# Four blocks of token tiles instead of three in a decoder step: samples in the second, recurrence over eight heads, weight stream opened per stage group

## The reference, cut to what matters

```
h = rms_norm(x, n_mix_pre) * (1 + sc1) + sh1
bg, cg, hin, q, k, v, r, ga, gb, alow = split(h @ w_in)
branch_a = (bg * short_conv(cg * hin)) @ w_proj_a
log_a = log_sigmoid(alow @ w_alpha + b_alpha) / 16
o, s_new = gla_chunked(q, k, v, log_a, state)       # recurrence over tokens, 4 heads
branch_b = (rms_norm(o) * silu(r)) @ w_proj_b
m = (sigmoid(ga) * branch_a + sigmoid(gb) * branch_b) @ w_out
x = x + g1 * rms_norm(m)
h = rms_norm(x) * (1 + sc2) + sh2
# PEER: 8 heads, two top-16 lists of 128 keys each, top 16 of the 256 sums = 128 experts a token
act = gelu(u_tab[expert] . h);  y = sum(gate * act * v_tab[expert])
x = x + g2 * rms_norm(y)
```

## Time and profile before

| | |
|---|---|
| device time, median of 3 runs | 4959.62 us (4947.52 to 4969.03) |
| the profiled execution | 4954.23 us, its span 4952.4 us |
| PE, DVE, POOL, ACT busy | 69%, 53%, 35%, 20% of the span |
| granted clock of PE, mean | 0.76 |
| DMA | 1454.19 MB, mean 294 GB/s |

### The profile page before, as it was taken

The page is one execution under the profiler, slowest core; times in us unless marked ns, Lnnn a source line. Parts: engine busy times, 40 slices in busy tenths (PEclk is TensorE's granted clock), DMA queues, the critical chain, the costliest instruction groups (busy, mean ns, idle before and its releaser), DMA issues. The chain is left out here.

```text
span 4952.4 us, 46615 instructions
## 1 busy us (share of the span) xinstructions
PE 3394.6 (69%) x15745; PEld 1770.1 (36%) x15745; DVE 2621.1 (53%) x7597; ACT 976.2 (20%) x1510; POOL 1735.2 (35%) x1393
## 2 busy tenths in 40 slices
PE   8694763449976676675688766666775566666666
PEld 2683563317643353341366523342430011111110
DVE  0224323874536544679546356545588655555555
ACT  1332123213233312210122333113210011000000
POOL 0460023325541134442355422344433233333332
PEclk9896576769987787787899977787786666666666
DMA  6552143359985578986799975689987899999998
GB/s 240 175 162 75 36 132 131 123 224 344 347 316 220 228 297 337 348 332 271 288 348 357 348 284 221 268 338 389 366 340 303 336 411 406 406 415 411 406 413 353
DMA packets 282043, 1454.19 MB, mean 294 GB/s; under 512 B 41143, under 2 KB 75063, under 8 KB 139598
## 3 DMA queue, kind: packets, MB, share of 16 engines
q0 software_dynamic: 156672, 1140.92, 58.2%
q1 hardware_dynamic: 125134, 310.31, 17.6%
HBM read 1386.30 MB, written 64.80 MB: 293 GB/s over the span
## 5 line engine op out<-in xcount | busy, mean ns | idle before, releaser
L559 DVE CUSTOM_DVE_ANT_0 peer_uv<-peer_uv,all_PS 128x512 f32<-128x512 f32 x2176 | 1439.2, 684 | 1286.1 <-PE all_PS L498 636.4
L481 POOL DMA_INDIRECT peer_uv<-in_uv,peer_idx x1088 | 1062.0, 976 | 2014.8 <-PE all_PS L517 1609.8
L498 PE MATMUL all_PS<-peer_hT,peer_sel 96*128 96x512 bf16 x2176 | 1001.2, 486 | 1024.0 <-DVE peer_halves L559 808.8
L369 POOL TENSOR_TENSOR flow_w_lo<-flow_w,flow_w_hi 128x1024 fp32r<-128x1024 f32 (+1 forms) x276 | 632.4, 2295 | 963.8 <-ACT flow_w_hi L362 963.0
L498 PEld LDWEIGHTS all_PS<-peer_hT,peer_sel 96*128 96x128 bf16 x2176 | 205.9, 103 | 1931.9 <-DVE peer_halves L559 1559.8
L517 PE MATMUL all_PS<-peer_uv,peer_zw 128*32 128x512 f32 x4352 | 854.7, 832 | 2.5 <-DVE peer_zw L579 2.5
L389 PE MATMUL all_PS<-mix_h_hi,flow_w_hi 128*128 128x384 f32 (+1 forms) x1056 | 413.2, 391 | 7.6 <-PE all_PS L749 3.6
L533 ACT ACTIVATE peer_ge<-peer_pre 128x4 f32<-128x4 f32 x272 | 55.8, 205 | 1780.6 <-DVE peer_pre L565 1778.8
L362 ACT ACTIVATE flow_w_hi<-flow_w 128x1024 fp32r<-128x1024 f32 (+1 forms) x276 | 279.4, 1018 | 564.7 <-DMA flow_w<-in_w_proj_a 120.0
L391 PE MATMUL all_PS<-mix_h_hi,flow_w_lo 128*128 128x384 f32 (+1 forms) x1056 | 353.8, 335 | 0.0
L390 PE MATMUL all_PS<-mix_h_lo,flow_w_hi 128*128 128x384 f32 (+1 forms) x1056 | 353.2, 334 | 0.0
(11 more groups left out here) (253 smaller groups left out, 4364.9 us busy)
## 6 DMA issues: line engine op xcount, KB each, us to landing
flow_w<-in_w_heads SPq DMA_DIRECT2D x72, 512.0 KB, 5.9
cond_w<-in_w_ada SPq DMA_DIRECT2D x12, 2048.0 KB, 8.4
flow_w<-in_w_gate_ab SPq DMA_DIRECT2D x48, 512.0 KB, 7.5
flow_w<-in_w_query SPq DMA_DIRECT2D x48, 512.0 KB, 5.6
flow_w<-in_w_conv SPq DMA_DIRECT2D x36, 512.0 KB, 6.7
peer_uv<-in_uv,peer_idx POOLq DMA_INDIRECT x1088, 9.5
flow_w<-in_w_proj_b SPq DMA_DIRECT2D x24, 512.0 KB, 5.7
flow_w<-in_w_out SPq DMA_DIRECT2D x24, 512.0 KB, 7.5
```

What stands on the lines that cost most here:

```text
L369: nc.gpsimd.tensor_tensor(self.lo[:, i % self.pairs, 0:nk], self.raw[:, i % self.raws, 0:nk], self.hi[:, i % self.pairs, 0:nk].bitcast(F32 ...
L481: self.nc.gpsimd.indirect_dma_start(out=self.uv[:, n % self.NUV, :], out_offset=None, in_=self.A["uv"], in_offset=bass.IndirectOffsetOnAxi ...
L498: nc.tensor.matmul(PS[:, f, :], self.sel[:, c:c + 1].broadcast_to([3 * GR, P]), self.hT[:, g % self.NH, f * 512:(f + 1) * 512], start=True ...
L559: nc.vector.tensor_tensor_reduce(part, part, PS[:, f, :], 1.0, 0.0, ALU.mult, ALU.add, self.halves[:, d, f, e:e + 1]).then_inc(M["dotted"], 1)
```

## The change

`ORDER` becomes 0, 1, 2, 3, samples, 4 to 7 and the blocks hold 2, 3, 2 and 2 tiles (256, 320, 256, 256 tokens); all that runs per block runs four times. Each block opens two streams, one in `mix_phase` and one in `merge_phase` for the four stages from there, and each begins its first four blocks inside its own stage. `SHARES` are given for blocks without and with samples. In `mix_phase` the sigmoids become tanh of half the value (sigmoid(x) = (1 + tanh(x/2)) / 2) with the rest done on DVE in `mix_phase` and `merge_phase`; of two prompt tiles, the second value step (`vb`) falls away. `chain_phase` treats the two prompt tiles as eight heads in one pipeline: gate logits of both tiles first, two exponent tiles `E`, heads ahead by two on PE and ACT, masks by halves, `sT`, `kT` twofold, results and state of a head one head later; the norm of the first tile is made among the heads of the second. Samples follow after it, with two state buffers in `room` that are saved and loaded again in turn. The masks of the pairs stay float32. `norm_phase` takes buffers of its own for the samples' rows instead of gather buffers and loads two of them late.

```diff
-ORDER = (0, 1, NT - 1) + tuple(range(2, NT - 1))
-EARLY = 2 * P
+ORDER = (0, 1, 2, 3, NT - 1) + tuple(range(4, NT - 1))
+EARLY = 4 * P
...
-BLOCKS = ((0, 3), (3, 6), (6, 9))
+BLOCKS = ((0, 2), (2, 5), (5, 7), (7, 9))
...
-                        nc.scalar.activation(out[:, p % 2, q, :], bank(j), ACT.Sigmoid).then_inc(a_out, 1)
+                        nc.scalar.activation(out[:, p % 2, q, :], bank(j), ACT.Tanh, scale=0.5).then_inc(a_out, 1)
...
-                    nc.vector.scalar_tensor_tensor(out=out[:, p % 2, tap_of, :], in0=bank(j), scalar=gnorm[:, 2 * c + tap_of:2 * c + tap_of + 1],
-                                                   in1=cg[:, :], op0=ALU.mult, op1=ALU.mult).then_inc(v_out, 1)
+                    step(nc.vector.tensor_scalar(cg[:, :], cg[:, :], 1.0, gnorm[:, 2 * c + tap_of:2 * c + tap_of + 1], ALU.add, ALU.mult))
+                    nc.vector.scalar_tensor_tensor(out=out[:, p % 2, tap_of, :], in0=bank(j), scalar=0.5, in1=cg[:, :],
+                                                   op0=ALU.mult, op1=ALU.mult).then_inc(v_out, 1)
...
-            for t in range(nt):
-                n, m0 = R[t], H * t
-                gat.spread(pe, turns.upto(10 * t))
...
-                exponents(m0)
-                for i in range(H):
-                    gat.spread(pe, turns.upto(10 * t + 1 + 2 * i))
...
-                    scores(m0 + i)
-                    if i + 1 < H:
-                        exponents(m0 + i + 1)
-                    gat.spread(pe, turns.upto(10 * t + 2 + 2 * i))
-                    results(m0 + i)
...
+            for t in range(NPT):
+                logits(t)
+            pe.wait_ge(M["masks_set"], 1)
+            for m in range(2):
+                for which in range(3):
+                    exponents(m, which)
+            gat.spread(pe, turns.upto(1))
+            for m in range(NPH):
+                t = m // H
+                gat.spread(pe, turns.upto(head_a(m)))
+                ahead = m + 2 if m + 2 < NPH else None
+                if m == 6:
+                    pe.wait_ge(M["squared"], 1)
+                    pe.wait_ge(M["masked"], 2 * m)
+                    norms(0)
+                if ahead:
+                    exponents(ahead, 0)
+                if m >= 2:
+                    pe.wait_ge(M["o_out"], m - 1)
+                turned(m)
...
+                scores(m, 0)
+                if ahead:
+                    exponents(ahead, 1)
+                    pe.wait_ge(M["t_out"], m + 1)
+                    exponents(ahead, 2)
+                gat.spread(pe, turns.upto(head_b(m)))
+                pe.wait_ge(M["masked"], 2 * m + 1)
+                scores(m, 1)
+                if m:
+                    pe.wait_ge(M["t_out"], m + 1)
+                    pe.wait_ge(M["e_exp"], 3 * min(m + 3, NPH))
+                    results(m - 1)
...
+                    sp.wait_ge(M["st_out"], sts(NPH + i + 1))
+                    sp.wait_ge(M["o_mm"], NPH + i + 1)
+                    sp.dma_start(A["out_gla_s"][i], Ss[i % 2]).then_inc(ss_saved[i % 2], 16)
+                    if i + 2 < H:
+                        sp.wait_ge(ss_saved[i % 2], 16)
+                        sp.dma_start(Ss[i % 2], A["state"][i + 2]).then_inc(ss_in[i % 2], 16)
...
             gat.fetch(pool, turns.before())
+            w.start(nc, pool=pool)
             for j in range(NJ):
...
-                nc.vector.tensor_tensor(sig[:, d % 2, q, :], bank(j), sig[:, d % 2, q, :], ALU.mult).then_inc(part_out, 1)
+                nc.vector.scalar_tensor_tensor(out=sig[:, d % 2, q, :], in0=sig[:, d % 2, q, :], scalar=1.0, in1=bank(j), op0=ALU.add,
+                                               op1=ALU.mult).then_inc(part_out, 1)
...
-SHARES = (170, 100, 50, 38, 42, 90, 100)
+SHARES = ((165, 115, 80, 40, 60, 80, 75), (190, 220, 90, 50, 70, 95, 100))
...
-                w = Stream(flow, once * len(PARTS))
...
+                        with Scope(nc, f"flow{part.index}") as flow:
+                            mix_phase(nc, A, G, part, gat, Stream(flow, early), 0, a_in, low, marks[0], marks[1])
+                        chain_phase(nc, A, G, part, gat, low, marks[1], marks[2])
+                    with Scope(nc, f"late{part.index}") as merging:
+                        w = Stream(merging, late)
+                        merge_phase(nc, A, G, part, gat, w, 0, a_in, marks[2], marks[3])
```

740 lines of the change are left out of this document (440 added, 300 removed).

## The result

The changed kernel takes 5115.18 us at the median (5111.91 to 5119.76, four runs) against 4959.34 (4947.52 to 4969.03) for the kernel before on the same chip: a ratio of 1.0316, 95% interval 1.0292 to 1.034. It is slower, by 156 us. The forecast was 5005, slower by 45; the direction was right and the time lies in the range of 4850 to 5140, but 111 of the 156 us were not in the sum. The profiled execution has a span of 5118.0 us.

The account below looks back on a forecast made before the run. No engine beats the DMA, so DMA busy plus idle time per block was summed: 150 + 696 + 1193 + 1204 + 1067 + 694 = 5004 us, stated as 5005 against a median of 4959.6; range 4850 to 5140.

Parts of the forecast that it names:

- The fourth pass against the last stage: Whole kernel: block 0 and the tail give back 581 us, a new block costs 633 net of the others' relief.
- DMA busy time: Blocks 1, 2, 3 beneath gather: 869, 1059 and 889 us, each with 140 us for the weight pass.
- Recurrence idle: DMA idle in the recurrence: 140, 20 and 40 us in blocks 1, 2, 3; heads 16 to 20 us apart in block 2.
- rival E: Recurrence: order on DVE keeps heads serial, +35 us a block in blocks 0 to 3, 5145 us; chance 0.07.
- Pick idle: DMA idle in the pick stage: 84, 35 and 48 us in blocks 1, 2, 3.
- The step that failed: DMA idle in the five stages besides recurrence and pick: 85 us in block 1, 75 each in blocks 2 and 3.
- openings: Weight streams begun inside projection and merge beneath gather: 8 us each, 15 a block; bounds nothing and 16 each, 96 for six.
- Tanh: Gates on ACT: fewer table reloads taken at nothing; bounds a gain of 38 us in two blocks and as much loss.
- the added DVE instruction: For each r block and each merged row: like the 0.5 us ones, under 10 us a block, hidden beneath DMA.
- B: Blocks beneath gather: gather fills idle time, 2.13 us a token, rest scaled by rows; 4780 to 4930, at 4870 us; chance 0.27.
- C: Openings and stage edges at upper bounds: 96 instead of 45, five stages keep 110; priced at 5110 us; chance 0.18.
- D: Block 0's projection: PE stays at the lower clock, 5.1 us a weight block against 3.65; 5143 us; chance 0.06.

Follow-up runs that it names:

- thin weights: Changed kernel loading one eighth of each weight block after each raw slot's first full one: 4970.5 us; same edit in the kernel before: 4879.2 us.
- split: Kernel before, cut into four blocks of 3, 2, 2, 2 tiles with nothing else of the change: 5138.76 us, ratio 1.036.

## Why the prediction was right in direction and wrong in size

**The fourth pass against the last stage.** Right in kind and on one side in size: block 0 and the last stage give back 578 us (forecast 581), and the blocks beneath gather cost 744 more than the two of before (forecast 633). The last stage is 2.76 us a token. Block 0 came within 10 us: recurrence 103 (110), pick 129 (121), projection 215.6 (215).

**DMA busy time.** Right for blocks 2 and 3 (+1, +12). Block 1 is 26 us over.

**Recurrence idle.** Block 1: 0.39 x 361 = 141, forecast 140. Block 2: 0.19 x 226 = 43 against 20. Block 3: 0.25 x 196 = 49 against 40. Its heads follow each other at 21 us in block 2, just over the 16 to 20 that was named; the 35 us a block of rival E are what undoing the pipeline costs.

**Pick idle.** 0.46 x 150 = 69 (84), 0.25 x 148 = 37 (35), 0.28 x 126 = 35 (48): 26 us over-priced in all.

**The step that failed.** "Seven barriers a block remain, while PE and DVE have a third less to do in a two-tile block: I judge 75 in these, 85 in block 1", with 15 a block for openings: 280 us of idle in the other five stages of three blocks. What is left of the measured idle after recurrence and pick is 348 - 141 - 69 = 138, 173 - 43 - 37 = 93 and 198 - 49 - 35 = 114, together 345, openings among it. Before, without these openings, they were 109 and 111 a block; with a mean of 115 they did not shrink by the third that I took off. 345 - 280 = 65 is the largest term of the miss, before the 33 of the recurrence and the 39 of DMA busy time. It is not spread evenly: block 1, which still has three tiles and was priced down all the same, has 38 of it, block 3 24 and block 2 3. The reason that the sum gave is not borne out, as far as it is PE's: with a third of its products left out no stage beneath gather got shorter (though the clock fell with them); DVE's share was not tested. What is idle there waits, as far as the traces show it, for landings and for the hand-over between PE and DVE. That a pass of 256 rows has as many of these as one of 384 would explain it; it is argued and not shown.

Behind this term lies a weaker premise: that a block is DMA busy time plus an idle time of its own. With thin weights the busy time of the hardware queue fell by 410 us (0.199 of 5118 to 0.122 of 4981.4), that of the gather's queue rose by 67 (0.566 to 0.595), and the time fell by 145. A sum of this kind can price an added pass only roughly, even with each idle term right.

All of it: 65 + 33 + 39 - 26 (pick) - 10 (to block 0's end) + 13 (last stage) = 114 = 5118 - 5004. (The forecast's last line has a slip: 5006 and the 5.4 us that it names are 5011, not 5005.)

Beside that I took the new shares into account for the recurrence alone and not for merge, where they put 42 and 33 tokens; 25 us of the miss go away with them. The openings that I priced at 45 for six come out at 5 for three merges and at 37 for five openings.

**Tanh** taken at nothing gave 20 us, inside its bounds of 38. The bounds themselves counted 30 loads at two lines; 77 went, about half of them at the gelu. And the added DVE instruction was priced as one of 0.5 us: it took 2.3 us in block 0, 18.4 us there and not under 10.

**Rivals.** B, the gather fills idle time for nothing: fallen, the shares stay at 0.72 to 0.86 and not at 0.96. Its slope of 2.13 us a token was near (2.09); its error was "without a fixed part": the part without tokens, scaled by rows and less 35 for the heads, was 426 us against the 564 of the line. C, openings and edges at their upper bounds, priced at 5110, is nearest in time, and part of that is luck: it had 330 + 96 = 426 us of idle where 345 were measured and the sum had 280, and the rest of the miss lies in the recurrence, the DMA busy time and the last stage. Its sign, POOL idle for over 15 us before the first split of a merge, is there if its waits are added up and just missed by the longest alone; in block 2's merge they are 14.93, 4.32 and 4.28 us, each before one of these rows:

```profile
2657.65 0.94 POOL L481 DMA_INDIRECT peer_uv<-in_uv,peer_idx  x1 [14.93 <-POOLq L109]
2662.91 0.94 POOL L481 DMA_INDIRECT peer_uv<-in_uv,peer_idx  x1 [4.32 <-PE all_PS L517]
2668.12 1.26 POOL L369 TENSOR_TENSOR late_w_lo<-late_w,late_w_hi 128x512 fp32r<-128x512 f32 x1 [4.28 <-ACT late_w_hi L362]
```

D, the clock: 0.92 in block 0's projection, not under 0.85; the two-level fall did not happen. The Trainium skill (TensorE: Matmul & The Clock Gate, HAM oscillation — how this bites in real kernels) has a thin group that waits on loads fall back to the slow clock; the trace of this stage does not show that: PE, busy 170 of 216 us, stayed mostly at full clock. Its waits there, after one of 29.6 us at the start, were 3.8 us at the longest. E, serial heads: fallen, the heads are pipelined, and its 35 us a block are what undoing that costs.

**How the change's parts add up** from the runs: split +179, heads -106, tanh -22, samples -4, openings +5 to +37, shares +25. That is +77 to +109 where +156 was measured. Some 47 to 79 us belong to no part tried alone, or to parts that cost more together. The prices of the parts were taken in different kernels (the split and the upper value of the openings in the kernel before, the rest in the changed one), and their sum need not come out.

## What to carry to other kernels

When work is cut into more passes beneath a saturating transfer, price the pass from two blocks that differ only in how much they cover (slope and rest), and don't scale that rest by rows; a block with nothing over it gives a check from above. Busy and idle time of the transfer trade against each other, so neither can be priced alone. A stage whose engines are all under 80% busy may still have two limits of the same height; relieve them one by one and each looks free. Before the tiling is changed, move the covered work between stages: 24 of 590 shares gave here some 40 us, which a rebuilt kernel did not.

## What the hardware showed beyond expectation

Loads of 512 KB on the hardware queue land in 3.5 us at the median without gather (block 0's projection), and beneath the gather's queue in about 7 to 10; a third and fourth in flight raise the median in block 3's projection from 7.0 to 8.4 and 8.8. An eighth of the bytes still takes 2.9 us there and 5.2 in block 2's, against 1.9 without gather: the time falls with the size, but by far less than the size does.

The TENSOR_SCALAR L822 of 128 x 256 on DVE takes 0.35 us, and up to 3.2 where POOL works on a TENSOR_TENSOR at the same time: in all 28 such cases of the changed kernel it ended 0.15 to 0.19 us after POOL's. A short instruction on an idle engine can thus cost what another engine's costs.

With a third of the products gone the mean granted clock over the run fell from 0.761 to 0.736 and the time stayed the same (5118.8 against 5115.2 us).

An ACT table load is 1.283 us in every row. 77 of them cost 22 us of the run in the changed kernel, 0.28 us each. The Trainium skill (ScalarE: Activation LUTs, What ACT_TABLE_LOAD costs) gives the same 1283 ns for the load and some 1380 ns of drain beside it, 2.66 us for a switch; the rows agree on the load, and no run here shows the drain by itself.
